# A second feed-forward's down projection with seven products of block sums in place of eight block products, on a quarter of its chunks

## The reference

```python
h = rms_norm(x, norm_mlp_pre)
u = jnp.square(jax.nn.relu(h @ w_up))            # 256 x 8192
x = x + rms_norm(u @ w_down, norm_mlp_post)      # 256 x 2048
```

## Time and profile before

| | |
|---|---|
| median of 3 runs | 2482.23 us |
| the profiled execution, its own time | 2482.3 us |
| its span in the trace | 2480.3 us |
| granted TensorE clock | 0.999 |
| busy, share of the span | TensorE 100%, VectorE 62%, ScalarE 49%, GpSimd 2% |
| chain that ended last | TensorE 99%, VectorE 1% |
| weight splits | 852 high parts of 1059 ns, 852 low parts of 1226 ns |
| read from memory | 468.85 MB, 190 GB/s over the span |

### The profile page before, as it was taken

How to read it: one execution, slowest core, us unless ns; L and a number is a source line. 1 busy time by engine, 2 the same in 40 slices (tenths; PEclk the granted TensorE clock), 3 DMA queues, 4 the chain that set the end, 5 groups by cost and what they waited for, 6 DMA issues and landing times.

```text
span 2480.3 us, 32951 instructions
## 1 busy us (share of the span) xinstructions
PE 2470.0 (100%) x12506; PEld 2095.2 (84%) x12506; DVE 1540.5 (62%) x1837; ACT 1218.8 (49%) x1574; POOL 47.2 (2%) x74
## 2 busy tenths in 40 slices
PE   9999999999999999999999999999999999999998
PEld 7888888888888888888888788888888888888887
DVE  5756767655777467755765457655665565564565
ACT  6444556545555355534554454445644443443443
POOL 0100100000000000000000000000000000000000
PEclk9999999999999999999999999999999999999999
DMA  9655565655655555555557555555465655555563
GB/s 326 209 188 175 163 177 171 221 187 170 205 188 193 197 187 186 187 203 187 186 188 261 155 189 180 163 168 178 145 223 191 193 192 188 191 194 190 188 210 128
DMA packets 251986, 472.57 MB, mean 191 GB/s; under 512 B 23344, under 2 KB 26928, under 8 KB 251232
## 3 DMA queue, kind: packets, MB, share of 16 engines
q1 hardware_dynamic: 251728, 470.98, 58.0%
q10 hardware_dynamic: 144, 0.03, 0.0%
HBM read 468.85 MB, written 2.13 MB: 190 GB/s over the span
## 4 chain that ended last, share of the span: by engine, by line
PE 99%; DVE 1%; ACT 0%; DMA 0%; issue 0%; DVEq 0%; POOLq 0%; POOL 0%; ACTq 0%
PE psum L2018 21%; PE psum L1927 20%; PE psum L1929 20%; PE psum L1928 20%; PE psum L2026 11%; PE psum L1983 1%; PE psum L1988 1%; PE psum L2043 1%; PE psum L2089 0%; PE psum L2111 0%; PE psum L2137 0%; PE psum L2079 0%; PE psum L1945 0%; PE psum L1944 0%; PE psum L1943 0%; PE psum L2402 0%
## 5 line engine op out<-in xcount | busy, mean ns | idle before, releaser
L1236 DVE TENSOR_TENSOR wl<-raw,wh 128x1024 fp32r<-128x1024 f32 x852 | 1041.5, 1226 | 851.3 <-ACT wh L753 848.9
L753 ACT ACTIVATE wh<-raw 128x1024 fp32r<-128x1024 f32 x852 | 893.4, 1059 | 955.3 <-PE psum L1929 587.6
L1927 PE MATMUL psum<-wh,ha 128*128 128x512 f32 x1696 | 673.7, 397 | 0.4 <-DVE ha L1405 0.4
L1929 PE MATMUL psum<-wh,ha 128*128 128x512 f32 x1696 | 661.4, 390 | 0.0
L1928 PE MATMUL psum<-wl,ha 128*128 128x512 f32 x1696 | 660.7, 390 | 0.0
L1929 PEld LDWEIGHTS psum<-wh,ha 128*128 128x128 f32 x1696 | 318.3, 188 | 68.0
L1927 PEld LDWEIGHTS psum<-wh,ha 128*128 128x128 f32 x1696 | 318.7, 188 | 65.5 <-issue 2.6
L1928 PEld LDWEIGHTS psum<-wl,ha 128*128 128x128 f32 x1696 | 319.0, 188 | 62.3
L2018 PE MATMUL psum<-ha,wh 128*128 128x512 f32 x1344 | 313.1, 390 | 0.0
L2018 PEld LDWEIGHTS psum<-ha,wh 128*128 128x128 f32 x1344 | 249.7, 188 | 50.1
L2018 PE MATMUL psum<-hb,wh 128*128 128x512 f32 x896 | 209.1, 390 | 0.0
(11 more groups left out here) (272 smaller groups left out, 1459.5 us busy)
## 6 DMA issues: line engine op xcount, KB each, us to landing
raw<-in_w_up SPq DMA_DIRECT2D x152, 1024.0 KB, 5.1
raw<-in_w_in SPq DMA_DIRECT2D x116, 1024.0 KB, 5.1
raw<-in_w_down SPq DMA_DIRECT2D x108, 1024.0 KB, 5.0
raw<-in_w_out SPq DMA_DIRECT2D x32, 1024.0 KB, 5.0
raw<-in_w_branch_a SPq DMA_DIRECT2D x8, 1024.0 KB, 4.9
raw<-in_w_branch_b SPq DMA_DIRECT2D x8, 1024.0 KB, 5.0
raw<-in_w_in SPq DMA_DIRECT2D x5, 512.0 KB, 7.7
x_t<-in_x_t SPq DMA_DIRECT2D x8, 256.0 KB, 6.1
```

The costliest lines, as they stand in the source:

```text
L753: act.activation(wh[q % SPLIT_SLOTS][:], raw[q // 2 % RAW_SLOTS][:, 2 * (q % 2):2 * (q % 2) + 2, :], ACT.Copy).then_inc(hi_done, 1)
L1236: dve.tensor_tensor(wl[q % SPLIT_SLOTS][:], raw[q // 2 % RAW_SLOTS][:, 2 * (q % 2):2 * (q % 2) + 2, :], wh[q % SPLIT_SLOTS][:].bitcast(F32 ...
L1927: pe.matmul(acc, hi, wh[s][:, c, :], start=first and c == 0, stop=False)
L1929: ins = pe.matmul(acc, lo, wh[s][:, c, :], start=False, stop=last and c == 1)
```

## The change

Take two column blocks together, a pair. The four steps of a pair that touch chunks 0 to 3 of the 16 (two for each block) are done as one 2x2 block product. A is the activations (two row tiles by two groups of two chunks), B the weights (two groups of chunks by two column blocks). Of eight block products A*B seven are left, made from sums of A and sums of B; a step of this kind has six matmuls, since one product covers one tile of rows. Chunks 4 to 15 stay as they were. So a pair has 19 steps instead of 16, in the order of `PAIR_STEPS`: six plain, seven of six matmuls, six plain; a pass has 70 steps instead of 64.

- **Sums of A**: once a pass, on VectorE, from the first up block's activations, with their own high part (ScalarE) and low part (VectorE).
- **Sums of B**: four a pair, on GpSimd (`weight_sum`), each of two 128x1024 operands in SBUF. Their loads stand fourth and fifth of the pair's eight (`PAIR_LOADS`), and their `raw` slots are held until the last of the seven is split.
- **The products**: three go straight into the banks of the plain steps, four into the other four banks; from these VectorE makes four sums which it adds to `y_rows` (`shared_products`), after one copy by ScalarE (`first_product`).
- **Order**: the first block of a pair is now closed in its fifteenth step and added four steps ahead of the pair's end; the loops of ScalarE and VectorE over passes are written out. A few semaphores are merged.

The core of the diff; left out are the helpers that number steps and loads, the renamed semaphores, SyncE's loop, and ScalarE's written-out loop, which keeps its order and takes `first_product` in the ninth step of a pair:

```diff
+PAIR_STEPS = [(0, 2), (0, 3), (0, 4), (0, 5), (1, 2), (1, 3)] + list(range(7))
+PAIR_STEPS += [(0, 6), (0, 7), (1, 4), (1, 5), (1, 6), (1, 7)]
+N_PAIR = len(PAIR_STEPS)
+SEVEN = PAIR_STEPS.index(0)
+PAIR_LOADS = [(0, 1), (0, 2), (1, 1), (0, 0), (1, 0), (0, 3), (1, 2), (1, 3)]
...
+    w_sum = [at(f"w_sum{i}", [P, 2, COLS], kb) for i, kb in enumerate((192, 196, 201, 205))]
+    a_sum = at("a_sum", [P, 4, 2, P], 172)
+    a_hi = at("a_hi", [P, 4, 2, P], 176, F32R)
+    a_lo = at("a_lo", [P, 4, 2, P], 180, F32R)
+    p_sum = [at(f"p_sum{i}", [P, COLS], 164 + 2 * i) for i in range(4)]
...
+        def weight_sum(p, pair, n):
+            u = LOADS_BEFORE + 32 * p + 16 + 8 * pair + 3
+            for v in (u, u + 1):
+                pool.wait_ge(raw_in[v % RAW_SLOTS], 16 * (v // RAW_SLOTS + 1))
+            (b11, b21), (b12, b22) = ([raw[v % RAW_SLOTS][:, 2 * k:2 * k + 2, :] for k in range(2)] for v in (u, u + 1))
+            made = 8 * p + 4 * pair
+            if made:
+                last = S_DOWN2[p] if pair else S_DOWN2[p - 1] + N_PAIR
+                pool.wait_ge(lo_done, last + SEVEN + 3 + n + 1)
+            if n == 2:
+                pool.wait_ge(sem["sum_ok"], made + 1)
+            if n == 3:
+                pool.wait_ge(sem["sum_ok"], made + 3)
+            plus, minus = ((b12, b11), (b22, b12), (b22, w_sum[0][:]), (b21, w_sum[2][:]))[n]
+            pool.tensor_tensor(w_sum[n][:], plus, minus, ALU.subtract).then_inc(sem["sum_ok"], 1)
+        for p in range(UP2_PASSES):
+            for pair in range(2):
+                for n in range(4):
+                    weight_sum(p, pair, n)
...
+            if q >= S_UP2[0]:
+                u, part = ff2_source(q)
+                act.wait_ge(mm_done, q - SPLIT_SLOTS + 1)
+                if u is None:
+                    act.wait_ge(sem["sum_ok"], sums_before(q) + part + 1)
+                    src = w_sum[part][:]
+                else:
+                    act.wait_ge(raw_in[u % RAW_SLOTS], 16 * (u // RAW_SLOTS + 1))
+                    src = raw[u % RAW_SLOTS][:, 2 * part:2 * part + 2, :]
+                act.activation(wh[q % SPLIT_SLOTS][:], src, ACT.Copy).then_inc(hi_done, 1)
+                return
...
+                if c % 4 == 0:
+                    act.activation(a_hi[:], a_sum[:], ACT.Copy)
...
+        def first_product(p, pair):
+            act.wait_ge(mm_done, S_DOWN2[p] + N_PAIR * pair + SEVEN + 1)
+            dst = p_sum[0][:] if p else y_rows[:, 0, 2 * pair * COLS:(2 * pair + 1) * COLS]
+            act.activation(dst, psum[:, 4 - 4 * pair, :], ACT.Copy).then_inc(sem["first_copied"], 1)
...
+                ins = dve.scalar_tensor_tensor(u_act[:], u_sum[:], 0.0, u_sum[:], ALU.max, ALU.mult)
+                if c % 4 == 0:
+                    chain.link(ins)
+                    (a11, a12), (a21, a22) = ([u_act[:, 2 * k:2 * k + 2, P * t:P * t + P] for k in range(2)]
+                                              for t in range(NT))
+                    chain.link(dve.tensor_tensor(a_sum[:, 0], a21, a22, ALU.add))
+                    chain.link(dve.tensor_tensor(a_sum[:, 1], a_sum[:, 0], a11, ALU.subtract))
+                    dve.tensor_tensor(a_sum[:, 2], a11, a21, ALU.subtract)
+                    ins = dve.tensor_tensor(a_sum[:, 3], a12, a_sum[:, 1], ALU.subtract)
+                ins.then_inc(sem["act_ready"], 1)
             if j == 4:
-                dve.wait_ge(sem["hb_hi"], 11 + c + 1 + 4 * i)
+                dve.wait_ge(sem["hb_hi"], 11 + c + 1)
+                if c % 4 == 0:
+                    dve.tensor_tensor(a_lo[:], a_sum[:], a_hi[:].bitcast(F32), ALU.subtract)
...
+        def shared_products(p, pair, n):
+            bank = 4 - 4 * pair
+            e = [psum[:, bank + i, :] for i in range(4)]
+            (y11, y12), (y21, y22) = ([y_rows[:, t, (2 * pair + b) * COLS:(2 * pair + b + 1) * COLS]
+                                       for b in range(2)] for t in range(NT))
+            first, u2, u3, u4 = (p_sum[i][:] for i in range(4)) if p else (y11, p_sum[1][:], y21, y12)
+            if n == 0:
+                dve.wait_ge(mm_done, S_DOWN2[p] + N_PAIR * pair + SEVEN + 7)
+                dve.wait_ge(sem["first_copied"], 2 * p + pair + 1)
+                if p:
+                    dve.tensor_tensor(y11, e[0], y11, ALU.add)
+                chain.link(dve.tensor_tensor(u2, e[2], first, ALU.add))
+            if n == 1:
+                dve.tensor_tensor(u4, e[1], u2, ALU.add)
+                chain.link(dve.tensor_tensor(u3, e[3], u2, ALU.add))
+            if n == 2:
+                if p:
+                    dve.tensor_tensor(y21, u3, y21, ALU.add)
+                    dve.tensor_tensor(y12, u4, y12, ALU.add)
+                chain.link(dve.tensor_tensor(u2 if p else y22, e[1], u3, ALU.add))
+                dve.sem_inc(sem["extra_free"], 1)
+            if n == 3 and p:
+                chain.link(dve.tensor_tensor(y22, u2, y22, ALU.add))
+        def add_block(p, b, steps):
+            cols = slice(b * COLS, (b + 1) * COLS)
+            dve.wait_ge(mm_done, steps)
+            bank = row_bank(R_DOWN2[p] + b)
+            dve.tensor_tensor(y_rows[:, :, cols], psum[:, bank:bank + 2, :], y_rows[:, :, cols], ALU.add
+                              ).then_inc(row_free, 1)
+        for p in range(UP2_PASSES):
+            for r in range(PASS_STEPS):
+                if p == 0 and r < 8:
+                    if r < 3:
+                        add_tiles(5 + r)
+                    if r < 5:
+                        fill_lo(hb, T_MLP2, FIRST_FILLS + r, "mlp2")
+                if S_UP2[p] + r + AHEAD < N_STEPS:
+                    ahead(S_UP2[p] + r)
+                if 8 <= r < 40:
+                    up2_stage(r % 8, 4 * p + r // 8 - 1)
+                pair, n = divmod(r - 32, N_PAIR)
+                if pair >= 0:
+                    begin = S_DOWN2[p] + N_PAIR * pair
+                    if SEVEN + 7 <= n < SEVEN + 11:
+                        shared_products(p, pair, n - SEVEN - 7)
+                    if n == SEVEN + 11:
+                        add_block(p, 2 * pair, begin + SEVEN + 9)
+                if r == 51:
+                    add_block(p, 1, S_DOWN2[p] + N_PAIR)
+                if p == UP2_PASSES - 1 and r in (53, 57, 69):
+                    gain_rows(5, (53, 57, 69).index(r), 2)
+            if p < UP2_PASSES - 1:
+                add_block(p, 3, S_UP2[p + 1])
...
+        def seven_products(p, pair, q):
+            banks, shared = 4 * pair, 4 - 4 * pair
+            if pair:
+                pe.wait_ge(row_free, FREE + R_DOWN2[p] + 2)
+            else:
+                pe.wait_ge(chan_free, FREE + C_UP2[p] + 4)
+            def plain(t, half):
+                return [[ha[:, 2 * half + c, part, P * t:P * t + P] for part in range(2)] for c in range(2)]
+            def summed(n):
+                return [[part[:, n, c, :] for part in (a_hi, a_lo)] for c in range(2)]
+            products = [(plain(0, 0), shared, True), (plain(0, 1), banks, False), (summed(3), banks + 2, False),
+                        (summed(0), shared + 1, True), (summed(2), shared + 3, True), (summed(1), shared + 2, True),
+                        (plain(1, 1), banks + 1, False)]
+            for n, (chunks, bank, alone) in enumerate(products):
+                pe.wait_ge(lo_done, q + n + 1)
+                s, acc = (q + n) % SPLIT_SLOTS, psum[:, bank, :]
+                for c, (hi, lo) in enumerate(chunks):
+                    pe.matmul(acc, hi, wh[s][:, c, :], start=alone and c == 0, stop=False)
+                    pe.matmul(acc, hi, wl[s][:, c, :], start=False, stop=False)
+                    ins = pe.matmul(acc, lo, wh[s][:, c, :], start=False, stop=alone and c == 1)
+                ins.then_inc(mm_done, 1)
         rows_before = R_OUT2 + 4
         for p in range(UP2_PASSES):
             peeled = 1 if p == 0 else 0
+            if p:
+                pe.wait_ge(sem["extra_free"], 2 * p)
             channel_blocks(S_UP2[p] + 16 * peeled, C_UP2[p] + 2 * peeled, 2 - peeled, hb, rows_before)
             pe.wait_ge(chan_free, FREE + C_UP2[p] + 3)
-            for b in range(4):
-                g = R_DOWN2[p] + b
-                pe.wait_ge(row_free, g + 1)
-                if b == 2:
-                    pe.wait_ge(chan_free, FREE + C_UP2[p] + 4)
-                ends = g == R_DOWN2[-1] + 3
-                for j in range(4 if ends else 8):
-                    hb_by(11 + 4 * p, 4)(j)
-                    rows_step(S_DOWN2[p] + 8 * b + j, 0, 0, ha, (2 * j, 2 * j + 1), g, j == 0, j == 7)
+            for pair in range(2):
+                q, g = S_DOWN2[p] + N_PAIR * pair, R_DOWN2[p] + 2 * pair
+                if pair:
+                    pe.wait_ge(sem["extra_free"], 2 * p + 1)
+                ends = (p, pair) == (UP2_PASSES - 1, 1)
+                for n, step in enumerate(PAIR_STEPS):
+                    if isinstance(step, tuple):
+                        b, j = step
```

(8 more changed lines are left out.)

155 lines of the change are left out of this document (82 added, 73 removed).

## The result

The changed kernel takes 2486.82 us (median of 20 runs, 2485.86 to 2487.91). The kernel before, beside it on the same chip, takes 2482.48 (20 runs, 2482.05 to 2482.91). The ratio is 1.0018, 95% interval 1.0011 to 1.0024: 4.3 us slower. The forecast was 2484.4, range 2474 to 2491. The profiled execution took 2486.84 us (span 2485.1, granted clock 0.998; before it was 0.999), against 2482.3 (span 2480.3). Its span is 4.8 us longer, and the traces say where.

The account below looks back on a forecast made before the run. TensorE, busy 100% of the span, was taken as the bound. Against 2482.3 us: - 10.9 (matmuls removed) + 3.5 (end) + 9.6 (GpSimd's sums) = + 2.2, so 2484.4 by the median; range 2474 to 2491.

Parts of the forecast that it names:

- Removed: In each pair, four steps of twelve matmuls become seven of six: 48 matmuls fewer, 10.9 us off TensorE.
- The port: First pair of each pass: GpSimd's sums and VectorE's instructions exclude each other, 2.4 us lost a pass, 9.6 in all.
- the first rival: Each GpSimd sum shuts VectorE out longer, 2.6 us: loss 3.9 us a pass, time 2490.4; chance 0.27.
- No exclusion at all: GpSimd gives way or finds VectorE's gaps, so TensorE feels nothing: loss 0, time 2474.8 us; chance 0.15.
- VectorE keeps the port: VectorE goes on back to back, GpSimd's sums wait for its gaps: loss 0.8 us a pass, 2478.0; chance 0.13.
- The tail: After the last low part, VectorE's extra additions and the third column block's own delay the end by 3.5 us.
- VectorE's and ScalarE's added work: Three more splits, eight additions and one copy a pair, four activation sums and their split a pass: cost nothing.
- that cover: First up block of a pass: slack that hides the activation sums; without it up to 1 us a pass.
- about 0.6 us before it is due: First up block of a pass: its last step's split, delayed by the activation sums, still in time; cost nothing.
- no difference: Whole kernel: about 0.2% (5 us) is what a measurement can tell from no change, 2477.3 to 2487.2; chance 0.52.
- my bound for slower: Whole kernel: a time above 2487.2 us counts as slower; chance 0.27.

## Why the prediction held, and where it did not

**Removed, 10.9 us: as said.** 48 matmuls less, and where TensorE isn't held up a down stage takes 84.32 us (six kernels), 2.72 less than 87.04.

**The port, 9.6 us: as said, measured 10.6.** ("The port" is the prediction's name for what the rows show, that the two engines shut each other out.) Hold: sum 0 can have the port once the low part at 2387.74 has let it go, at 2387.74 + 1.07 = 2388.81 (its 1.23 us less the 0.16 between release and recorded end). The low part issued at 2390.46 lasts 1.85 for 1.23 of work, so it got its input at 2391.08. The hold is 2.27 us, where I took 2.22; the longer hold of the first rival (from 2.39) is out. The turns came as laid out: `u_act` at t = 15.9 (15.8), TensorE's steps 6 to 8 late, step 8 at 21.5 (21.45), no second pair late. A pass lost 2.64, not 2.4: step 8's delay is 2.46 of it, and most of the rest lies inside step 8, whose fourth matmul starts at 2408.77, 0.82 behind its first instead of 0.68. The three kernels without the loss gave back 9.5 us (constants in place of sums), 9.7 (sums on VectorE) and 9.7 (half sums) in the medians, each with a spread of about 1 us to either side; the stages' starts say 4 x 2.64 = 10.6. In the profiled executions the spans are 9.3, 9.9 and 10.6 us shorter. What the first two lack is mostly the later row scales of pass 0 (1.3 and 0.3 us by the table above), and for the second 0.4 us that stood ahead of that stretch.

**The other rivals.** No exclusion at all is ruled out by the stretched rows, and by the two kernels in which GpSimd adds nothing and nothing is lost. That VectorE keeps the port when its next instruction is queued is ruled out by L1940: it was queued directly behind a low part, and GpSimd's sum still went first. The 0.08 us that spoke against it in the earlier trace rows told the truth. The rows show how: L1940's record starts at 2392.24, while the low part before it let go at 2391.08 + 1.07 = 2392.15, so the next instruction of the same engine is there only when the waiting one is already in.

**The tail, 3.5 us: as said, measured 3.6.** The end grew by 3.64 us. Tile 1's last addition starts 3.65 us later against the last matmul (4.28 - 0.63), and the chain between the two tiles is 5.20 as it was. Counted from the last low part (2462.78 before, 2463.93 after), the forecast had the block's addition 3.8 us behind it, where it is 3.90, the gain 6.5, where it is 6.67, and tile 0's last addition 8.2, where it is 8.36.

**VectorE's and ScalarE's added work, "nothing": wrong in pass 0, 1.3 us.** I had written "without that cover up to 1 us a pass" and that the last split of the first up block comes "about 0.6 us before it is due". That was worked out from the pace of the splits, not from the rows of pass 0. In pass 0 the cover is already spent, because VectorE waits there for the row scales' DMA (5.14 us in the trace above, 4.52 in the kernel before). Down stages and the other up stages took the added work for nothing, as said. (In pass 0 it is four additions a pair and not eight, since its sums are stored and not added to `y_rows`; at a price of nothing that changes no number.)

**The sum.** - 10.9 + 10.6 + 3.6 + 1.3 = + 4.6, and 0.2 that stood ahead of all of it make the span's 4.8. The forecast had + 2.2: of the 2.4 us between, 1.3 are the step that was priced at nothing, 1.0 the port, 0.1 the tail. All three err to the same side. By the medians it is 2486.8 against 2484.4, and the 0.18% is real (the interval leaves out 1), though it is less than the 0.2% that I had called no difference. That it stayed under 2487.2, my bound for slower, is in part luck: the step priced at nothing cost 2.7 us in the profile of another kernel with the same stretch, and 5 of the 20 runs lie above the bound.

## What to carry to other kernels

Work that is moved to an idle engine isn't free where it and a busy one shut each other out of memory, as these two do here: price the hold, and lay it out hand over hand against the queue of the busy engine. Here 32 sums on an engine that was busy 2% cost 10.6 us, and the same sums in the queue of the one that was busy 62% cost nothing. Here the cost had a threshold: at half the width, or in a pair without the up block in the queue, it was zero. And slack is read at each place where the pattern stands, the first above all: here the row scales came late there, and later in some executions than in others.
